# Retention blocks of a decoder step: the sample's state update moved behind the next block's low parts, and the last head's low parts moved to VectorE

## The chip, the core and the metric

The kernel runs on one core of a Trainium2 chip. The engines are TensorE (PE in the profile, PEld for its weight loads), VectorE (DVE), ScalarE (ACT), GpSimd (POOL) and SyncE (SP, which here only issues transfers). Each engine works through its own instructions in order and waits on semaphores. The metric is the device time of one execution in microseconds (us), as the median of three runs.

## What is computed

The reference is a decoder trunk of two layers for a prompt of 1024 positions and eight samples of one position. Layer 0 is windowed attention, layer 1 is retention, and each layer ends in a gated ConvFFN. The change touches the retention alone, and in it this recurrence (a chunk is 128 positions for the prompt, 1 for a sample; there are 4 heads, keys of 256 and values of 512):

```python
def step(s, inp):
    qi, ki, vi = inp
    inner = jnp.einsum('bihd,bjhd->bhij', qi, ki) * decay_in
    o = jnp.einsum('bhij,bjhe->bihe', inner, vi)
    o = o + jnp.einsum('bihd,bhde->bihe', qi, s) * q_decay[None, :, :, None]
    s = s * chunk_decay[None, :, None, None] + jnp.einsum('bjhd,bjhe->bhde', ki * k_decay[None, :, :, None], vi)
    return s, o
...
o = ((o - mu) * lax.rsqrt(var + GN_EPS)).reshape(b, t, nv)
out = (jax.nn.silu(g) * o).astype(x.dtype) @ w_o
```

The samples' states `state_ret` (8 samples, 4 heads, 256 x 512 each) are decayed, get the outer product of key and value added, go back to memory, and are multiplied with the sample's query.

## The kernel before, in words

Every large product is done in two parts: an operand is split into a high part (ScalarE, a copy that rounds) and a low part (VectorE or GpSimd, the operand less its high part), and TensorE adds three products: high x high, low x high, high x low.

The retention runs over 32 blocks `i` (head `h = i // 8`, chunk `n = i % 8`), and in block `i` one sample's state of that head is handled too: there are 8 samples and 8 chunks. Each engine has a function `period(i)`, in which the order of its work is written out by hand; `i` runs from 0 to 33, the last two without a live block. Between the block's own steps TensorE does filler jobs (a job is a product of 24 matmuls of 128 x 344 in blocks 0 to 15, in halves of 12, and of 12 such matmuls from block 16 on); `fill(i, s)` does those of slot `s`. From block 16 on a block has four or five jobs in turn.

TensorE in `period(i)`: `fill(i, 0)`; `inner(i)` (query times key; waits for the low parts of the key, `k_lo`); `back(i - 1)`; `update(i, 0)`; `fill(i, 1)`; `update(i, 1)` (waits until VectorE has taken up `update(i, 0)`); `fill(i, 2)`; `output(i)`; `turn(i + 1)` (the transposes of the next block); `fill(i, 3)`; `sample_out(i - 1)` (the sample's query times its new state, line 1359; waits for the semaphore `outer`); `fill(i, 4)`.

VectorE: the adds of finished jobs in the `fill` slots; `decayed(i)`, `gated(i - 1)`, `update(i, 0)`, `inner_lo(i)`, `update(i, 1)`; low parts of weight slabs in `split_planned` (line 2081), by a plan that says how many units each slot gets; `outer(i - 1)` (line 2752, two instructions of 128 x 512: state = value x key + state, both inputs in SBUF); `norm(i)` and `norm_rest(i)` (group norm of the block's output); `rows(i + 1)` (lines 2717 and 2719: the low parts of the next block's values and keys, `r_vl` and `r_kdl`); two more slots with adds and low parts of slabs.

ScalarE: `inner_hi(i)`; `decay(i)` (line 1926: the sample's state times its decay; waits for the load); high parts of slabs; `sample_state_out(i - 1)` (line 1938, issues the store of the state; waits for `outer`); `values_hi(i + 1)`; `state_hi(i)` (high parts of the prompt's state); more high parts of slabs (line 1428).

GpSimd: `heads_lo` (line 3094: low parts of finished heads `xl`, two instructions a call); `queries_lo(i + 1)`; `state_lo(i)` (line 3086: low parts of the prompt's state, 128 x 1024, both inputs in SBUF; not in the last chunk of a head).

SyncE loads the state of sample `i + 1` (`sample_state`, two buffers; waits for `sample_out` of the sample before and for the store that used the buffer) and the values (`sample_values`, one buffer) and then the next queries and values of the prompt.

Behind the blocks comes `last_chunks`: TensorE does two jobs, then `mean(6)` (line 839), which waits until GpSimd has added up eight tiles of `y` in `sums` (lines 3002 and 3005).

Of the kernel before, what the change touches and what calls it, by code (L numbers as in the profile page):

```python
# [459 lines left out]
def planned_slabs(i, k):  # L460
# [11 lines left out]
            "inv probs pt pt_in heads heads_hi heads_lo kv_out win_out s_sc s_scc "  # L472
            "s_tr s_mx s_ex s_p s_pt s_ptc s_o s_of s_oh s_ol dchain").split()
RET_SEMS = ("m_in dec_in cq0 cq1 cv cg0 cg1 turned q_hi q_lo v_hi v_lo k_hi k_lo inner inn i_hi i_lo kv state out_ "
            "s_hi s_lo stats small root ga back ob o_out o_hi o_lo st_in0 st_in1 st_out0 st_out1 decay outer "
            "x_in x_ing masks rows x_part x_sum xv xv_out vb x_o x_stats x_small x_root x_ga x_back xo xo_hi xo_lo "
            "s_out oin0 oin1 oin2").split()

# [1 line left out]
def own_columns(ch):  # L480

    return slice(ch * CH, min((ch + 1) * CH, SEQ))
# [315 lines left out]
def tensor_engine(pe, K):  # L798
# [461 lines left out]
    def ret_out(key):  # L1260

        h = key[1] if key[0] == "o" else RH - 1
        ch, ft = divmod(key[2], KT)
        s = S_O + 4 * h + ft // 2
        if ch == 0 and ft % 2 == 0:
            wait_slab(pe, S, s)
        if ft == 0:
            pe.wait_ge(R["o_lo"], 2 * (NCH * h + ch) + 2)
            if ch == NCH - 1:
                pe.wait_ge(R["xo_lo"], h + 1)  # L1270
        if key == ("o3", 0, 12):
            pe.wait_ge(R["state"], 2 * NI)
        free(key)
        c, out, terms = columns(ch), bank[BANK[key]][:, 0:CH], []
        for k in range(4):
            f = slice((2 * k + ft % 2) * P, (2 * k + ft % 2 + 1) * P)
            x = (4 * h + k) % KT
            w_hi, w_lo = unit_hi_lo(K, UNIT_OF_SLAB[s])
            terms.append((w_hi[:, f], w_lo[:, f], xh[:, x, c], xl[:, x, c]))
        accumulate(pe, out, terms).then_inc(S["jobs"], 1)  # L1280

    def fill(i, s):

        if i < MIXED:
            if s < 4:
                ret_half(FILL[i][s // 2 * 2 + 1][0], s % 2)
            return
        for key in FILL[i][s]:
            ret_out(key)
# [59 lines left out]
    def sample_out(i):  # L1349
        h, b = divmod(i, NB)  # L1350
        pe.wait_ge(R["masks"], h + 1)
        pe.wait_ge(R["outer"], 2 * i + 2)
        if b == 0:
            after(pe, R["x_sum"], h)
        for half in range(2):
            c = slice(half * RV // 2, (half + 1) * RV // 2)
            for j in range(2):
                at = 32 * (2 * half + j)
                mm = pe.matmul(xB[at:at + NS, c], K.qm[:, j, b, :], K.s0[:, i % 2, j, c], start=(b == 0), stop=(b == NS - 1))
        mm.then_inc(R["x_o"], 1)  # L1360
# [9 lines left out]
    def period(i):  # L1370
        h, n = divmod(i, NB)
        live = i < NI
        fill(i, 0)
        if live:
            inner(i)
        if 1 <= i <= NI:
            back(i - 1)
        if live:
            update(i, 0)
        fill(i, 1)  # L1380
        if live:
            update(i, 1)
            if n == 0:
                rows(h)
        if i in SAMPLES_BACK:
            sample_back(SAMPLES_BACK.index(i))
        fill(i, 2)
        if live:
            output(i)
        if i + 1 < NI:  # L1390
            turn(i + 1)
        fill(i, 3)
        if 1 <= i <= NI:
            sample_out(i - 1)
        fill(i, 4)

    for g in range(NG):
# [9 lines left out]
def scalar_engine(act, K):  # L1407
# [515 lines left out]
    def decay(i):  # L1923
        h = i // NB
        act.wait_ge(R[f"st_in{i % 2}"], 16 * (i // 2) + 16)
        act.activation(K.s0[:, i % 2, :, :], K.s0[:, i % 2, :, :], ACT.Copy, scale=K.dec[:, h % 2, W + 4:W + 5])\
            .then_inc(R["decay"], 1)
# [44 lines left out]
    def fill(jobs):  # L1972
        for key in jobs:
            if key[0] == "p":
                project(*key[1:])

    def period(i):
        h, n = divmod(i, NB)
        live = i < NI
        fill(FILL[i][0])  # L1980
        if live:
            inner_hi(i)
        if 1 <= i <= NI:
            gated_out(i - 1)
        if n == 1 and h:
            sample_parts(h - 1)
        if i == NI + 1:
            sample_root(RH - 1)
        fill(FILL[i][1])
        if live:  # L1990
            decay(i)
            if n == 0:
                sample_rows(h)
        if i in HEADS_SPLIT[:-1]:
            heads_hi(HEADS_SPLIT.index(i))
        if i < NI:
            split_planned(i, 1)
        elif FILL[i][1]:
            split_upto(J[FILL[i][1][-1]], U_F1)
        fill(FILL[i][2])  # L2000
        if 1 <= i <= NI:
            sample_state_out(i - 1)
        if n == 2 and h and live:
            sample_root(h - 1)
        if i in SAMPLES_PUT:
            sample_put(SAMPLES_PUT.index(i))
        if i == HEADS_SPLIT[-1]:
            heads_hi(len(HEADS_SPLIT) - 1)
        if live and n == NB - 1:
            state_out(h)  # L2010
        if i + 1 < NI:
            queries_hi(i + 1)
        if live:
            heads_root(i)
        if i + 1 < NI:
            values_hi(i + 1)
        if live and n < NB - 1:
            state_hi(i)
        if MIXED <= i < NI:
            split_planned(i, 2)  # L2020
        fill(FILL[i][3])
        if i < NI:
            split_planned(i, 3)
        fill(FILL[i][4])
        if i < NI:
            split_planned(i, 4)
        elif FILL[i][4]:
            split_upto(J[FILL[i][4][-1]], U_F1)
        if i == NI + 1:
            split_upto(J[FILL[i][3][-1]], U_F1 + 2)  # L2030
# [37 lines left out]
def vector_engine(dve, K):  # L2068
# [743 lines left out]
    def sample_put(h):  # L2812
        dve.wait_ge(R["xo_hi"], h + 1)
        k, c = sample_place(h)
        dve.tensor_tensor(xl[:, k, c], K.xo[:, :, :], xh[:, k, c].bitcast(F32), ALU.subtract).then_inc(R["xo_lo"], 1)

    def fill(jobs):
        for key in jobs:
            if key[0] == "p":
                project(*key[1:])  # L2820
            else:
                add(key)

    def period(i):
        h, n = divmod(i, NB)
        live = i < NI
        if i == NI + 1:
            sample_sums(RH - 1)
            sample_norm(RH - 1)
        fill(FILL[i][0])  # L2830
        if live:
            decayed(i)
        if 1 <= i <= NI:
            gated(i - 1)
        if live:
            update(i, 0)
            inner_lo(i)
        if i == NI + 1:
            sample_norm_rest(RH - 1)
        fill(FILL[i][1])  # L2840
        if live:
            update(i, 1)
        if n == 1 and live:
            if h:
                sample_sums(h - 1)
            masks(h)
        if n == 2 and h and live:
            sample_norm(h - 1)
        if i < NI:
            split_planned(i, 1)  # L2850
        elif FILL[i][1]:
            split_upto(J[FILL[i][1][-1]], U_F1)
        if 1 <= i <= NI:
            outer(i - 1)
        fill(FILL[i][2])
        if n == 2 and h and live:
            sample_norm_rest(h - 1)
        if i in SAMPLES_BACK:
            sample_gated(SAMPLES_BACK.index(i))
        if live:  # L2860
            norm(i)
        if i in SAMPLES_PUT:
            sample_put(SAMPLES_PUT.index(i))
        if live:
            norm_rest(i)
        if i + 1 < NI:
            rows(i + 1)
        if MIXED <= i < NI:
            split_planned(i, 2)
        fill(FILL[i][3])  # L2870
        if i < NI:
            split_planned(i, 3)
        fill(FILL[i][4])
        if i < NI:
            split_planned(i, 4)
        elif FILL[i][4]:
            split_upto(J[FILL[i][4][-1]], U_F1)
        if i == NI + 1:
            split_upto(J[FILL[i][3][-1]], U_F1 + 2)
# [54 lines left out]
def pool_engine(pool, K):  # L2934
# [161 lines left out]
    def period(i):  # L3096
        n = i % NB
        fill(FILL[i][0])
        if i in HEADS_SPLIT[:-1]:
            heads_lo(HEADS_SPLIT.index(i))  # L3100
        fill(FILL[i][1] + FILL[i][2])
        if i + 1 < NI:
            queries_lo(i + 1)
        if i < NI and n < NB - 1:
            state_lo(i)
        if i == HEADS_SPLIT[-1]:
            heads_lo(len(HEADS_SPLIT) - 1)
        fill(FILL[i][3] + FILL[i][4])

    pool.memset(K.eps[:, :], EPS).then_inc(S["e_in"], 1)  # L3110
# [43 lines left out]
def sync_engine(sp, K):  # L3154
# [193 lines left out]
    def period(i):  # L3348
# [8 lines left out]
            slabs_to(min(due_by(J[(FILL[i - 1][4] or FILL[i - 1][3])[-1]]), S_F1) + RAW)  # L3357
        if live:
            gates(i)
        if i == 14:  # L3360
            heads_written(8)
            sp.wait_ge(S["jobs"], J["p", 3, 11, 0])
            heads(0, 0)
# [32 lines left out]
        if i == 33:  # L3396
            heads_written(NI)
            heads_landed(2, 3)
            heads(3, 2)
        if i + 1 < NI:  # L3400
            sample_state(i + 1)
        if live:
            sample_values(i)
        if i == 15:
            sp.wait_ge(S["jobs"], J["p", 3, 11, 1])
            heads(0, 1)
# [209 lines left out]
```

## Time and profile before

| | us |
|---|---|
| median of three runs (lowest, highest) | 2744.42 (2742.86, 2746.85) |
| the profiled execution: its own time | 2740.04 |
| its span in the trace | 2738.0 |
| busy: PE | 2661.2 (97%) |
| busy: DVE | 1780.2 (65%) |
| busy: ACT | 1095.2 (40%) |
| busy: POOL | 767.0 (28%) |

A share is that of the span. Busy times add up each engine's own instructions; TensorE's matmuls overlap one another, so its row says when it had work and not how fast it was. A wait stands in the trace as the idle time in front of an instruction, with the instruction that ended it.

### The profile page before, as it was taken

What the parts mean: (1) busy time and instruction counts of PE and PEld (TensorE: products, weight loads), DVE (VectorE), ACT (ScalarE), POOL (GpSimd) and SP (SyncE); (2) the same over time, 40 slices, a digit from 0 to 9 for tenths busy, and PEclk for the clock granted to TensorE, in tenths of its full rate; (3) what the DMA queues carried; (4) which work ended last, traced back from release to release, by engine and by line L of the source; (5) the groups of instructions that cost most, each with busy time, mean ns of one, the idle gap of its engine ahead of it and who ended that gap; (6) DMA issues with size and microseconds to landing.
All of it is one profiled execution on the core that took longest, in us unless ns stands there. A gap on an engine that the chain in (4) does not pass through costs nothing.

```text
span 2738.0 us, 48829 instructions
## 1 busy us (share of the span) xinstructions
PE 2661.2 (97%) x19550; PEld 2549.9 (93%) x19550; DVE 1780.2 (65%) x3270; ACT 1095.2 (40%) x2089; POOL 767.0 (28%) x603
## 2 busy tenths in 40 slices
PE   8999989999999999999999999999899999999997
PEld 7888879999999999999999888898799999999997
DVE  6556578676767445766463675877688666766455
ACT  5445455433343122643434435433264444342123
POOL 3344351322220002354241232332341223220021
PEclk9999999999999999999999999999999999999999
DMA  4210111222224232123235777776502221223321
GB/s 141 82 48 11 40 33 55 70 86 78 84 79 155 70 116 65 67 93 122 96 109 173 220 233 220 232 224 199 162 22 73 82 82 70 86 96 123 114 73 62
DMA packets 182576, 290.83 MB, mean 106 GB/s; under 512 B 24976, under 2 KB 131088, under 8 KB 182320
## 3 DMA queue, kind: packets, MB, share of 16 engines
q1 hardware_dynamic: 152112, 251.65, 28.5%
q10 hardware_dynamic: 30240, 36.07, 3.7%
q8 instruction: 156, 2.56, 0.4%
q14 instruction: 68, 0.56, 0.1%
HBM read 206.82 MB, written 82.93 MB: 106 GB/s over the span
## 4 chain that ended last, share of the span: by engine, by line
PE 86%; DVE 6%; issue 3%; ACT 2%; POOL 1%; DMA 1%; ACTq 0%; SPq 0%; POOLq 0%; DVEq 0%
PE bank L1085 13%; PE bank L1087 13%; PE bank L1086 13%; PE bank L792 12%; PE bank L794 12%; PE bank L793 11%; PE bank L825 2%; PE bank L827 2%; PE bank L826 2%; PE bank L946 1%; PE bank L925 1%; DVE r_s L2752 1%; DVE wl L2081 1%; PE bank L936 1%; ACT wh L1428 0%
## 5 line engine op out<-in xcount | busy, mean ns | idle before, releaser
L2081 DVE TENSOR_TENSOR wl<-raw,wh 128x512 fp32r<-128x512 f32 (+1 forms) x460 | 428.9, 936 | 307.6 <-ACT wh L1428 302.5
L1428 ACT ACTIVATE wh<-raw 128x512 fp32r<-128x512 f32 (+1 forms) x492 | 344.3, 714 | 408.9 <-PE bank L794 224.7
L1085 PE MATMUL bank<-xh,wh 128*128 128x258 f32 x1792 | 506.7, 283 | 0.0
L1087 PE MATMUL bank<-xh,wl 128*128 128x258 f32 x1792 | 506.2, 282 | 0.0
L1086 PE MATMUL bank<-xl,wh 128*128 128x258 f32 x1792 | 505.5, 282 | 0.0
L1086 PEld LDWEIGHTS bank<-xl,wh 128*128 128x128 f32 x1792 | 338.7, 189 | 0.0
L1085 PEld LDWEIGHTS bank<-xh,wh 128*128 128x128 f32 x1792 | 338.2, 189 | 0.0
L1087 PEld LDWEIGHTS bank<-xh,wl 128*128 128x128 f32 x1792 | 337.9, 189 | 0.0
L2113 DVE TENSOR_TENSOR y<-bank,y 128x344 f32<-128x344 f32 x384 | 192.1, 512 | 218.4 <-PE bank L794 217.4
L3021 POOL TENSOR_TENSOR raw<-raw 128x512 f32<-128x512 f32 x56 | 72.1, 1287 | 742.8 <-DVE wl L2081 742.5
L1085 PE MATMUL bank<-x_t2h,wh 128*128 128x258 f32 x896 | 253.4, 283 | 2.0 <-ACT f_ab L1655 2.0
L1086 PE MATMUL bank<-x_t2l,wh 128*128 128x258 f32 x896 | 253.2, 283 | 0.0
L1087 PE MATMUL bank<-x_t2h,wl 128*128 128x258 f32 x896 | 252.7, 282 | 0.0
L1655 ACT ACTIVATE f_ab<-bank 128x258 f32<-128x258 f32 x224 | 86.1, 385 | 270.8 <-PE bank L1087 268.1
L1085 PEld LDWEIGHTS bank<-x_t2h,wh 128*128 128x128 f32 x896 | 169.1, 189 | 2.3 <-DVE wl L2081 2.3
L1087 PEld LDWEIGHTS bank<-x_t2h,wl 128*128 128x128 f32 x896 | 169.4, 189 | 0.0
L1086 PEld LDWEIGHTS bank<-x_t2l,wh 128*128 128x128 f32 x896 | 169.3, 189 | 0.0
L792 PE MATMUL bank<-xh,wh 128*128 128x344 f32 x488 | 163.0, 334 | 2.4 <-DVE f_cv L2392 1.5
L825 PE MATMUL bank<-xh,wh 128*128 128x344 f32 x472 | 156.4, 331 | 3.0 <-DVE xl L2150 2.3
L794 PE MATMUL bank<-xh,wl 128*128 128x344 f32 x488 | 157.0, 322 | 0.0
L793 PE MATMUL bank<-xl,wh 128*128 128x344 f32 x488 | 156.9, 321 | 0.0
L1655 ACT ACTIVATE f_g<-bank 128x258 f32<-128x258 f32 x224 | 84.1, 379 | 181.3 <-PE bank L1087 181.3
(308 smaller groups left out, 7192.8 us busy)
## 6 DMA issues: line engine op xcount, KB each, us to landing
raw<-in_w SPq DMA_DIRECT2D x216, 512.0 KB, 3.8
scratch_h<-f_g SPq DMA_DIRECT2D x40, 516.0 KB, 2.7
h_in<-scratch_h SPq DMA_DIRECT2D x30, 688.0 KB, 5.1
r_s<-in_state_in SPq DMA_DIRECT2D x32, 512.0 KB, 3.8
out_state_s<-r_s ACTq DMA_DIRECT2D x32, 512.0 KB, 3.5
scratch_qkvg<-f_ab SPq DMA_DIRECT2D x16, 516.0 KB, 4.1
scratch_qkvg<-f_g SPq DMA_DIRECT2D x16, 516.0 KB, 5.3
r_cxq<-scratch_qkvg SPq DMA_DIRECT2D x32, 256.0 KB, 5.4
```

Source lines behind the costliest of these rows:

```text
L792: pe.matmul(out, ah, bh, start=(k == 0), stop=False)
L793: pe.matmul(out, ah, bl, start=False, stop=False)
L794: mm = pe.matmul(out, al, bh, start=False, stop=(k == n - 1))
L825: pe.matmul(out, ah, xh[:, k, c], start=(k == 0), stop=False)
L1085: pe.matmul(out, hi[:, kk], bh, start=(k == 0 and not adds), stop=False, skip_group_check=adds)
L1086: pe.matmul(out, hi[:, kk], bl, start=False, stop=False, skip_group_check=adds)
L1087: mm = pe.matmul(out, lo[:, kk], bh, start=False, stop=(k == 3), skip_group_check=adds)
L1428: act.activation(hi, source, ACT.Copy).then_inc(S["hi_done"], 1)
L1655: act.activation(out, bank[PRODUCT_BANKS[sub][n]][:, 0:TQ], ACT.Copy).then_inc(S[f"copied{sub}"], 1)
L2081: dve.tensor_tensor(lo, source, hi.bitcast(F32), ALU.subtract).then_inc(S["lo_done"], 1)
L2113: dve.tensor_tensor(t, bank[b][:, 0:CH], t, ALU.add).then_inc(S["yadd"], 1)
L3021: pool.tensor_tensor(g[:, two], g[:, one], g[:, two], ALU.add).then_inc(S["w_sum"], 1)
```

## The change

The sample's part of a block is shifted, and the last low parts of the heads change their engine.

- VectorE: `outer(i - 1)` stands behind `rows(i + 1)`, no longer ahead of `norm(i)`.
- TensorE: `sample_out` stands in the next period, behind `fill(i, 0)` and ahead of `inner(i)`.
- ScalarE: `sample_state_out(i - 1)` and `decay(i)` stand behind slot 3, ahead of the slab parts of slots 3 and 4.
- SyncE: the state of sample `i` is loaded in period `i`, the values of sample `i - 1` in period `i` behind the gates.
- The last call of `heads_lo` goes from GpSimd to a new function `last_heads_lo` on VectorE, with a semaphore of its own, `o_end`. `sample_gated` stands ahead of the adds of slot 2.

```diff
@@ tensor engine, ret_out
         if ft == 0:
-            pe.wait_ge(R["o_lo"], 2 * (NCH * h + ch) + 2)
+            if (h, ch) == (RH - 1, NCH - 1):
+                pe.wait_ge(R["o_end"], 2)
+            else:
+                pe.wait_ge(R["o_lo"], 2 * (NCH * h + ch) + 2)
@@ tensor engine, period
         fill(i, 0)
+        if 2 <= i:
+            sample_out(i - 2)
         if live:
             inner(i)
...
         fill(i, 3)
-        if 1 <= i <= NI:
-            sample_out(i - 1)
         fill(i, 4)
@@ scalar engine, period
         fill(FILL[i][1])
-        if live:
-            decay(i)
-            if n == 0:
-                sample_rows(h)
+        if live and n == 0:
+            sample_rows(h)
...
         fill(FILL[i][2])
-        if 1 <= i <= NI:
-            sample_state_out(i - 1)
...
         fill(FILL[i][3])
+        if 1 <= i <= NI:
+            sample_state_out(i - 1)
+        if live:
+            decay(i)
         if i < NI:
             split_planned(i, 3)
@@ vector engine
+    def last_heads_lo():
+        n = NCH * RH - 1
+        for half in range(2):
+            k, c = slice(4 + 2 * half, 6 + 2 * half), own_columns(NCH - 1)
+            dve.wait_ge(R["o_hi"], 2 * n + half + 1)
+            dve.tensor_tensor(xl[:, k, c], xl[:, k, c].bitcast(F32), xh[:, k, c].bitcast(F32), ALU.subtract)\
+               .then_inc(R["o_end"], 1)
@@ vector engine, period
+        fill(FILL[i][0])
         if i == NI + 1:
             sample_sums(RH - 1)
             sample_norm(RH - 1)
-        fill(FILL[i][0])
...
-        if 1 <= i <= NI:
-            outer(i - 1)
+        if i in SAMPLES_BACK:
+            sample_gated(SAMPLES_BACK.index(i))
         fill(FILL[i][2])
         if n == 2 and h and live:
             sample_norm_rest(h - 1)
-        if i in SAMPLES_BACK:
-            sample_gated(SAMPLES_BACK.index(i))
         if live:
             norm(i)
         if i in SAMPLES_PUT:
             sample_put(SAMPLES_PUT.index(i))
+        if i == NI + 1:
+            last_heads_lo()
         if live:
             norm_rest(i)
         if i + 1 < NI:
             rows(i + 1)
+        if 1 <= i <= NI:
+            outer(i - 1)
         if MIXED <= i < NI:
             split_planned(i, 2)
@@ GpSimd, period
-        if i == HEADS_SPLIT[-1]:
-            heads_lo(len(HEADS_SPLIT) - 1)
@@ SyncE, period
         if live:
             gates(i)
+        if 1 <= i <= NI:
+            sample_values(i - 1)
...
-        if i + 1 < NI:
-            sample_state(i + 1)
-        if live:
-            sample_values(i)
+        if 1 <= i < NI:
+            sample_state(i)
```

VectorE in block 5, before (`r_il` is `inner_lo(5)`, `r_state` the second `update(5, 1)`, `r_s_145` the sample's state of `outer(4)`, `BN_STATS` the start of `norm(5)`):

```order
L2728 TENSOR_TENSOR r_il<-r_inn,r_ih 128x128 [waits r_i_hi]
L2742 SCALAR_TENSOR_TENSOR r_state<-r_state,r_dec,bank 128x512 [waits r_s_lo,r_kv]
L2752 SCALAR_TENSOR_TENSOR r_s_145<-r_vb,r_k_156,r_s_145 128x512 [waits r_vb,r_decay]
L2752 SCALAR_TENSOR_TENSOR r_s_145<-r_vb,r_k_156,r_s_145 128x512
L2768 BN_STATS r_st_139<-bank 128x6 [waits r_out_]
```

VectorE at the end of block 5 now (`r_vl` and `r_kdl` are the low parts of block 6's values and keys, `p_prod` the rotation of a filler job):

```order
L2785 TENSOR_SCALAR r_ga<-bank,r_st 128x512 [waits r_back,r_small]
L2720 TENSOR_TENSOR r_vl<-bank,r_vh 128x512 [waits r_v_hi]
L2722 SCALAR_TENSOR_TENSOR r_kdl<-bank,r_dec,r_kdh 128x256 [waits r_k_hi]
L2755 SCALAR_TENSOR_TENSOR r_s_145<-r_vb,r_k_156,r_s_145 128x512 [waits r_vb,r_decay]
L2755 SCALAR_TENSOR_TENSOR r_s_145<-r_vb,r_k_156,r_s_145 128x512
L2615 TENSOR_TENSOR p_prod<-bank,cosR 128x344 [waits rot,jobs]
```

The outer products have gone from ahead of the norm to between the low parts of the next block's keys and the filler's rotation.

TensorE at the end of block 4, before (`L1359` is `sample_out(3)`, the rows around it filler jobs):

```order
L827 MATMUL bank<-xh,wl 128x344
L1359 MATMUL bank<-r_s_145,r_qm 8x256 [waits r_outer,r_masks]
L1359 MATMUL bank<-r_s_145,r_qm 8x256 x3
L825 MATMUL bank<-xh,wh 128x344 [waits plain]
L826 MATMUL bank<-xl,wh 128x344
```

TensorE at the start of block 5 now (`L1362` is `sample_out(3)`, `L1315` `inner(5)`, `L1324` `back(4)`):

```order
L827 MATMUL bank<-xh,wl 128x344
L1362 MATMUL bank<-r_s_145,r_qm 8x256 [waits r_outer,r_masks]
L1362 MATMUL bank<-r_s_145,r_qm 8x256 x3
L1315 MATMUL bank<-r_cxq 128x128 [waits r_k_lo]
L1315 MATMUL bank<-r_cxq 128x128
L1324 MATMUL bank<-ident,r_ga 128x128 [waits r_v_lo,r_ga]
```

The product stands half a job (12 matmuls) later, directly ahead of `inner`; the outer products for which it waits now stand on VectorE behind the low parts for which `inner` waits.

ScalarE at the end of block 3, before (`r_sh` is `state_hi(3)`, `p_plain` a filler's result, `wh` the high part of a slab, `r_ih` `inner_hi(4)`):

```order
L1966 ACTIVATE r_sh<-r_state 128x1024 [waits r_out_,r_state]
L1783 ACTIVATE p_plain<-bank 128x344 [waits out_p1,jobs]
L1785 DMA scratch_qkvg<-p_plain 128x344 [waits plain]
L1428 ACTIVATE wh<-raw 128x1024 [waits jobs,raw_in0]
L1906 ACTIVATE r_ih<-r_inn 128x128 [waits r_inn]
```

ScalarE at the same place now (`L1941` is the store of the sample's state, `L1929` the decay):

```order
L1969 ACTIVATE r_sh<-r_state 128x1024 [waits r_out_,r_state]
L1786 ACTIVATE p_plain<-bank 128x344 [waits out_p1,jobs]
L1788 DMA scratch_qkvg<-p_plain 128x344 [waits plain]
L1941 DMA out_state_s<-r_s_145 128x1024 [waits r_outer]
L1929 ACTIVATE r_s_145<-r_s_145,r_dec 128x1024 [waits r_st_in1]
L1431 ACTIVATE wh<-raw 128x1024 [waits jobs,raw_in0]
L1909 ACTIVATE r_ih<-r_inn 128x128 [waits r_inn]
```

The store and the decay stand ahead of the slab's high part.

## Rows read from the trace of the kernel before

**Rows 1.** Waits of TensorE, 1495 to 2000 us: total us, times, longest us.

```profile
PE bank L839 <- POOLq L3009: 8.5, 1, 8.5
PE bank L1312 <- DVE r_kdl L2719: 6.2, 3, 3.6
PE bank L792 <- DVE r_state L2742: 5.9, 5, 1.7
PE bank L1304 <- DVE r_xo L2809: 2.8, 3, 1.3
PE bank L1359 <- DVE r_s L2752: 1.3, 1, 1.3
PE bank L1304 <- DMA r_cxq<-scratch_qkvg: 1.2, 1, 1.2
PE bank L792 <- issue: 0.9, 1, 0.9
PE bank L1367 <- DVE r_xv L2802: 0.3, 1, 0.3
```

**Rows 2.** Timeline, TensorE, blocks 6 and 7: start us, us, instruction [idle before].

```profile
1580.46 0.62 PE L1359 MATMUL bank<-r_s,r_qm 128*8 128x256 f32 x8
...
1582.99 0.60 PE L1312 MATMUL bank<-r_cxq 128*128 128x128 f32 x4
...
1586.45 0.39 PE L792 MATMUL bank<-r_vh,r_kdh 128*128 128x512 f32 x1
```

**Rows 3.** Timeline, VectorE, GpSimd and TensorE, from block 30 to block 31.

```profile
1936.47 0.47 DVE L2719 SCALAR_TENSOR_TENSOR r_kdl<-bank,r_dec,r_kdh 128x256 fp32r<-128x256 f32 x1
...
1936.54 2.40 POOL L3086 TENSOR_TENSOR r_sl<-r_state,r_sh 128x1024 fp32r<-128x1024 f32 x1 [1.99 <-ACT r_sh L1966]
...
1938.20 0.60 PE L1312 MATMUL bank<-r_cxq 128*128 128x128 f32 x4
```

**Rows 4.** Timeline, VectorE and GpSimd, blocks 30 and 31.

```profile
1930.00 1.41 DVE L2752 SCALAR_TENSOR_TENSOR r_s<-r_vb,r_k,r_s 128x512 f32<-128x512 f32 x2
...
1937.44 2.57 DVE L2081 TENSOR_TENSOR wl<-raw,wh 128x1024 fp32r<-128x1024 f32 x1 [0.49 <-ACT wh L1428]
...
1944.10 4.22 DVE L2752 SCALAR_TENSOR_TENSOR r_s<-r_vb,r_k,r_s 128x512 f32<-128x512 f32 x2
...
1944.01 3.75 POOL L3094 TENSOR_TENSOR xl<-xl,xh 128x688 fp32r<-128x688 f32 x2 [5.08 <-ACT xh L1917]
```

**Rows 5.** Timeline, VectorE and TensorE, block 29 with five jobs, into block 30.

```profile
1921.34 0.47 DVE L2719 SCALAR_TENSOR_TENSOR r_kdl<-bank,r_dec,r_kdh 128x256 fp32r<-128x256 f32 x1
...
1924.97 0.61 PE L1312 MATMUL bank<-r_cxq 128*128 128x128 f32 x4
```

**Rows 6.** Timeline, ScalarE, VectorE and TensorE, block 13.

```profile
1670.09 1.06 ACT L1428 ACTIVATE wh<-raw 128x1024 fp32r<-128x1024 f32 x1 [0.46 <-ACT p_plain L1783]
...
1674.58 1.15 ACT L1926 ACTIVATE r_s<-r_s,r_dec 128x1024 f32<-128x1024 f32 x1 [0.40 <-ACT p_plain L1783]
...
1671.18 1.22 DVE L2081 TENSOR_TENSOR wl<-raw,wh 128x1024 fp32r<-128x1024 f32 x1 [2.84 <-ACT wh L1428]
...
1674.01 0.47 PE L792 MATMUL bank<-r_vh,r_kdh 128*128 128x512 f32 x1 [1.32 <-DVE r_state L2742]
```

**Rows 7.** Timeline, GpSimd, the end of the blocks.

```profile
1968.75 4.28 POOL L3094 TENSOR_TENSOR xl<-xl,xh 128x672 fp32r<-128x672 f32 x2 [7.85 <-ACT xh L1917]
...
1975.03 6.16 POOL L3005 TENSOR_TENSOR n_ms<-n_ms,y 128x344 f32<-128x344 f32 x6
```

**Rows 8.** Windows on TensorE: stretch, us, busy (instructions), granted clock, DMA share, GB/s.

```profile
1640.60:1644.00 3.40, 3.40 (x13) 0.50 0.66 198
1715.70:1719.10 3.40, 3.40 (x13) 0.50 0.86 281
1763.60:1767.00 3.40, 3.38 (x20) 1.00 0.96 313
...
1981.30:1985.30 4.00, 4.00 (x12) 0.50 0.00 0
```

More of the change, by code:

```diff
@@ L474 @@
 RET_SEMS = ("m_in dec_in cq0 cq1 cv cg0 cg1 turned q_hi q_lo v_hi v_lo k_hi k_lo inner inn i_hi i_lo kv state out_ "
-            "s_hi s_lo stats small root ga back ob o_out o_hi o_lo st_in0 st_in1 st_out0 st_out1 decay outer "
+            "s_hi s_lo stats small root ga back ob o_out o_hi o_lo o_end st_in0 st_in1 st_out0 st_out1 decay outer "
             "x_in x_ing masks rows x_part x_sum xv xv_out vb x_o x_stats x_small x_root x_ga x_back xo xo_hi xo_lo "
```

## The prediction
> **What bounds the kernel now.** I read the page's busy times first: TensorE has work for 97% of the span, so a change in the order of the other engines can only move the idle time of TensorE. The view of who waited for whom on TensorE, for the stretch of the retention blocks, is therefore the budget [rows 1]: 8.5 us at `mean(6)`, where GpSimd's sums are late, and 18.6 us in the other seven rows, in waits of at most 3.6 us; 27.1 us in all. To that comes what the clock costs: behind the 8.5 us wait the granted clock is 0.50 (1.2 of 2.4 GHz) for 4.0 us, and it was 0.50 for 3.4 us in each of two stretches behind a wait for `r_kdl` [rows 8]. Work at half clock loses half its time, so these cost 2.0 + 1.7 + 1.7 = 5.4 us. Even if every one of these waits went and no new one came, 27.1 + 5.4 = 32.5 us is all that there is to win.
>
> Then I read the timeline of one boundary between two blocks on three engines, since the change puts a new link there. All times below count from k, the start of `r_kdl`, VectorE's last low part for the next block. TensorE begins `inner` at k + 1.73 (1938.20 less 1936.47), in a block with five jobs at k + 3.63 (1924.97 less 1921.34) [rows 3, 5]. GpSimd's `state_lo` begins at k + 0.07 and ends at k + 2.47 [rows 3]: exactly behind the low parts the port to SBUF is taken. What that does to VectorE is seen in two rows: the low part of a slab that starts in it takes 2.57 us and ends at 1940.01, 1.07 behind GpSimd's end; and two outer products beside two `heads_lo` instructions take 4.22 us where a pair alone takes 1.41, and end 0.56 behind GpSimd's end (1948.32 against 1947.76) [rows 3, 4]. So an instruction of VectorE with both inputs in SBUF makes hardly any way until GpSimd is done, and then needs most of its own time.
>
> **The change, part by part.** *The end of the blocks.* GpSimd loses its last `heads_lo`, 4.28 us ahead of the sums, of which six take 6.16 us in a row [rows 7]. Freed of it, it can add each tile soon after VectorE has added the job, one sum (1.03 us) per job of 1.9 us; the last sum then comes about a microsecond behind the last add, before TensorE has done its two jobs. The whole wait of 8.5 us and the 2.0 us of slow clock go. VectorE takes the low parts over; it waits there for jobs anyway, and TensorE needs `o_end` some nine jobs later: nothing.
>
> *The waits that go with the outer products.* They leave the place ahead of the norm, `sample_gated` moves ahead of an add, and queries are loaded earlier, since SyncE no longer stands at a wait for a late product. I let all of the other rows of the budget go, 18.6 us and 3.4 us of slow clock; where the same cause makes a wait again, it is counted below. Gain in all: 32.5 us.
>
> *The product now waits.* `sample_out` stands ahead of `inner` and takes some 0.6 us [rows 2], so TensorE comes to it at k + 1.73 - 0.6 = k + 1.13. The outer products follow `r_kdl`, inside `state_lo`. The first ends 0.56 behind it, at k + 3.03; the second adds 0.7 (half of 1.41): k + 3.73, and with some 0.1 for the semaphore TensorE goes on at k + 3.83. That is a wait of 2.7 us. Lower bound of this price: if GpSimd held nothing, the outer products would end at k + 0.4 + 1.41 = k + 1.8, and the wait would be 0.8. Upper bound: if each of the two were held as long as in the row of 4.22 us, they would end at k + 4.6 and the wait would be 3.6. I take 2.7, since `state_lo` is one instruction and can hold the pair but once. The plan of the jobs gives 21 boundaries of this kind (those with `state_lo` and four jobs, or two halves: from block 1 into 2 up to block 30 into 31): 21 x 2.7 = 56.7 us. Six boundaries follow a block with five jobs: TensorE comes at k + 3.63 - 0.6 and waits 0.8: 4.8 us. At two boundaries between heads there is no `state_lo`; the price is the lower bound, together 1.9 us. Sum 63.4 us. That the norm starts earlier without the outer products ahead of it helps little: in most blocks it waits for TensorE's output, and the boundary is counted from k in any case.
>
> Here a rule of the Trainium skill bears on the change. SBUF — State Buffer, section "Who interferes with whom", says that an instruction of VectorE with two SBUF inputs contends with a GpSimd instruction that reads SBUF, that whichever issues first keeps the shared ports for its whole length, and that the other one blocks fully. The rows agree for GpSimd ahead of VectorE; by the rule, the other order would hold `state_lo` instead, and the sum would be that of the first rival.
>
> *Store and decay ahead of the slab's high part.* ScalarE now waits for the outer products (k + 3.8), issues the store (0.4, the idle time that a store leaves in front of the decay), decays (1.15) and only then makes a high part of slots 3 and 4 (1.06) [rows 6]: ready at k + 6.4. VectorE's low part follows, and behind it stand `decayed`, `gated` and `update(i, 0)`, for which TensorE's second update waits: in block 13 it started 2.83 us behind the start of the low part [rows 6], so now at k + 9.3. Without that TensorE would be there 3.46 us behind `inner` [rows 2], at k + 3.83 + 0.6 + 3.46 = k + 7.9. A wait of 1.4 us at the five boundaries with a unit in slot 3 in the first half, 1.8 where an add lies between (three), 0.7 at the last of one head: 13.1 us. Below nothing it cannot fall; the upper end is the longest of the chain's own rows, 2.8 a time.
>
> *The last sample.* Its product stands one job later, with one job instead of two ahead of `sample_back`, which came only just too late before (0.3 us, [rows 1]). A job of 12 matmuls is 1.9 us (from the end of the product to `inner`, [rows 2]): 2.2 us.
>
> *Clock.* The 22 waits of 2.2 us and more are new, and the clock fell behind waits of 2.4 and 3.6 us, but not behind one of 1.7 [rows 1, 8]. One fall costs 1.7 us. Ends: none falls, 0; each falls, 37 us. These waits lie on the side of those with a fall, but each has a full block of work around it, so I take three in four: 28 us, less 5 where the slow stretch covers the 1.4 us wait for the slab: 23 us.
>
> *Nothing:* the load of a sample's state, though it moves a period back on SyncE. The store is issued at k + 3.8, and the next decay of that buffer stands a whole stretched block later; store and load take their turns in between. The loads of queries and values behind it on SyncE start earlier than before.
>
> **Sum.** 63.4 + 13.1 + 2.2 + 23 = 101.7 us lost, 32.5 us won: 69 us more. Against the profiled execution's own time of 2740.0 us that is 2809 us; the median of the runs lies 4.4 us above that execution, so I forecast 2814 us, 2.5% slower.
>
> **Rivals.**
> 1. *VectorE gets the port first.* If the outer products begin ahead of `state_lo`, GpSimd waits and not they. It decides itself by 0.33 us: `state_lo` would have to start behind k + 0.4 and not at k + 0.07. The price at the 21 boundaries falls to 0.8 us (16.8), at those with five jobs to nothing, and no clock falls: 16.8 + 1.9 + 13.1 + 2.2 - 32.5 = 1.5 us, so 2746 us, no change or just faster. Against it: `state_lo` hangs on ScalarE's `state_hi`, and ScalarE's order up to there is left as it was. Chance 0.09.
> 2. *No clock falls*: 69 - 23 = 46 us more, 2790 us. For it: 1.7 us did not do it [rows 8]. Chance 0.15; the other end, each wait with a fall, is 2822 us and part of the forecast.
> 3. *The sums stay late*, because VectorE's adds stand behind its new low parts and the slabs: the 10.5 us stay, 2824 us. Chance 0.08.
> 4. *The load becomes the bound*: store and load of one buffer would have to take over a whole block, and each block would grow by more: beyond 2842 us. Chance 0.04.
> 5. *The boundary moves ahead of TensorE.* I count from k; but VectorE no longer has the outer products (1.41) ahead of the norm, and if its low parts come 2.7 us earlier against TensorE than now, the product finds them done and only the end remains won: 10.5 us faster, about 2734 us. Against it: the keys' low part needs TensorE's transposes, and the norm its output, which VectorE cannot hasten. Chance 0.03.
>
> **How the numbers follow.** The forecast has the remaining 0.61. Its own bounds, with 0.3 us either way at 27 boundaries (8 us), reach from 2790 - 8 to 2822 + 8. I widen that a little for what the product's price leaves open (0.2 us a time are 4 us more): 2772 to 2842, which takes in rivals 2 and 3 and leaves out the first, fourth and fifth, 0.16. A measurement of this kernel tells 0.2% (5.5 us) from no change. Slower: 0.61 + 0.15 + 0.08 + 0.04 and a little of the first rival, 0.89; the same 0.06 and faster 0.05, from the first and fifth.
>
> **What would show it.** In the waits of TensorE the row of `mean(6)` is gone, and a row of the product (line 1362) waiting for the outer products (line 2755) stands in its place, some 29 times, with 2.7 us as the usual wait and some 60 us in all. The outer products behind `r_kdl` show 3 us and more for a pair. The second update waits for `r_state` up to 2 us at eight or nine boundaries, `sample_back` over 2 us. The granted clock falls to 0.50 many times between 1500 and 2050 us. I am wrong if the pairs show 1.4 us there, or if TensorE's sum of waits in that stretch is under 50 us.

## The result, and the profile after

| | before | changed |
|---|---|---|
| median of four runs, us (lowest, highest) | 2743.64 (2740.75, 2746.85) | 2814.88 (2809.99, 2818.03) |
| span of the profiled execution | 2738.0 | 2811.7 |
| TensorE busy in it | 2661.2 | 2687.4 |

The changed kernel takes 1.0257 times as long (95% interval 1.0243 to 1.0271): 71 us more. Forecast were 69 us more and 2814 us. So small a miss proves little; the terms have to be held against the rows one by one.

The page of the changed kernel, its span and the busy times (us, share of the span, instructions):

```profile
span 2811.7 us, 48832 instructions
...
PE 2687.4 (96%) x19550; PEld 2574.3 (92%) x19550; DVE 1809.5 (64%) x3272; ACT 1096.4 (39%) x2089; POOL 758.4 (27%) x601
```

TensorE has the same 19550 instructions as before and is busy 26.2 us longer. The same work took longer; that this is the clock is shown below, by the run in which TensorE was kept busy through its waits. The waits of TensorE in the stretch of the blocks, 1495 to 2070 us (line, what it waited for, total us, times, longest us), answer to [rows 1]:

```profile
PE bank L1362 <- DVE r_s L2755: 60.9, 27, 3.2
PE bank L1362 <- issue: 4.4, 3, 2.7
PE bank L1370 <- DVE r_xv L2805: 2.5, 1, 2.5
PE bank L792 <- DVE r_state L2745: 2.3, 2, 1.4
PE bank L792 <- DVE r_state L2749: 1.6, 2, 1.3
```

Of the eight rows of before three are left: `r_state` (5.9, now 3.9, in other blocks), `sample_back` (`r_xv`, 0.3, now 2.5) and the product (line 1362), which had 1.3 us and now has 60.9 + 4.4 = 65.3; its three waits under "issue" are of the same kind. The 8.5 us at `mean(6)` and the waits for `r_kdl`, `r_xo` and `r_cxq` are gone. Ahead of this stretch one wait has grown for which the forecast had no term: the first block's `inner`, 3.7 us where it was 1.5.

```profile
PE bank L1315 <- DVE r_kdl L2722: 3.7, 1, 3.7
```

It belongs to no part of the change that I can name: the kernels tried below had it at anything from 2.4 to 4.3 us, and one and the same kernel showed 2.4 and 3.2. What sets it stays open.

The account closes: waits 71.7 + 3.7 now against 27.1 + 1.5 before are 46.8 us more, and with 26.2 us of busy time that is 73.0 of the 73.7 us that the span has grown.

The timeline of one boundary, block 5 into 6, on VectorE, GpSimd, TensorE and ScalarE (start us, us, instruction, idle time before):

```profile
1586.35 0.47 DVE L2722 SCALAR_TENSOR_TENSOR r_kdl<-bank,r_dec,r_kdh 128x256 fp32r<-128x256 f32 x1
1586.42 2.37 POOL L3099 TENSOR_TENSOR r_sl<-r_state,r_sh 128x1024 fp32r<-128x1024 f32 x1 [2.00 <-ACT r_sh L1969]
1586.74 3.25 DVE L2755 SCALAR_TENSOR_TENSOR r_s<-r_vb,r_k,r_s 128x512 f32<-128x512 f32 x2
...
1590.15 0.84 PE L1362 MATMUL bank<-r_s,r_qm 128*8 128x256 f32 x8 [2.60 <-DVE r_s L2755]
1590.45 1.15 ACT L1929 ACTIVATE r_s<-r_s,r_dec 128x1024 f32<-128x1024 f32 x1 [4.10 <-DVE r_s L2755]
```

This is the link that the forecast described: k is 1586.35, GpSimd's low part of the state begins 0.07 later, and the pair of outer products takes 3.25 us and ends at k + 3.64 (forecast k + 3.73). TensorE waits 2.60 us. And the clock, as windows on TensorE (stretch, us, busy and instructions, granted clock, DMA share, GB/s), first the blocks of the kernel before, then the changed kernel:

```profile
1500.00:1990.00 490.00, 462.33 (x2911) 0.98 0.68 211
...
1500.00:2040.00 540.00, 471.82 (x2826) 0.94 0.59 189
...
1590.41:1593.81 3.40, 3.40 (x19) 0.50 0.64 234
1655.27:1662.10 6.83, 6.17 (x27) 0.50 0.40 129
```

Right behind the wait that ended at 1590.15 the granted clock is 0.50, 1.2 GHz, for 3.4 us; over the whole stretch it is 0.94 where it was 0.98 before. The same view behind each of the product's 21 waits of 2.6 to 3.2 us shows such a fall in 16 places. In three of them, the last row above among them, the clock stays at 0.50 for 6 us and more. Behind the other five waits, all of 2.60 to 2.62 us, it stays at 1.00; what decides between them is open.

### The profile page after: what moved, and what is told of

It reads as the page before. It is cut to its first block, busy times and chain, and to the rows that moved or that the text cites. A ratio compares the mean times of both kernels' runs of the same rounds, so it can differ in the third digit from the quotient of the medians.

```text
span 2811.7 us, 48832 instructions
## 1 busy us (share of the span) xinstructions
PE 2687.4 (96%) x19550; PEld 2574.3 (92%) x19550; DVE 1809.5 (64%) x3272; ACT 1096.4 (39%) x2089; POOL 758.4 (27%) x601
## 4 chain that ended last, share of the span: by engine, by line
PE 83%; DVE 10%; issue 3%; ACT 2%; DMA 1%; POOL 1%; SPq 0%; ACTq 0%; POOLq 0%; DVEq 0%
PE bank L1085 13%; PE bank L1087 13%; PE bank L1086 13%; PE bank L792 12%; PE bank L794 11%; PE bank L793 11%; DVE r_s L2755 3%; PE bank L825 2%; PE bank L827 2%; PE bank L826 2%; PE bank L1315 1%; PE bank L946 1%; PE bank L925 1%; PE bank L1362 1%; DVE r_vl L2720 1%
## 5 line engine op out<-in xcount | busy, mean ns | idle before, releaser
L2084 DVE TENSOR_TENSOR wl<-raw,wh 128x512 fp32r<-128x512 f32 (+1 forms) x460 | 422.5, 922 | 309.0 <-ACT wh L1431 303.2
```

The source lines that it names most:

```text
L2084: dve.tensor_tensor(lo, source, hi.bitcast(F32), ALU.subtract).then_inc(S["lo_done"], 1)
```

## The experiments

A ratio is to the kernel before, run in the same comparison. Over the five comparisons the median of the kernel before was 2742.51 to 2744.57 us, so medians of kernels from different comparisons are also set beside each other here. Some 0.2% (5.5 us) can be told from nothing. Diffs are against the changed kernel, where nothing else is said.

### The end of the blocks alone

The kernel before, with `last_heads_lo` on VectorE in place of GpSimd's last call, and TensorE's wait for `o_end`; nothing of the shift.

```diff
         if i in SAMPLES_PUT:
             sample_put(SAMPLES_PUT.index(i))
+        if i == NI + 1:
+            last_heads_lo()
...
-        if i == HEADS_SPLIT[-1]:
-            heads_lo(len(HEADS_SPLIT) - 1)
```

> The kernel before, with nothing of the change but the last head's low parts on VectorE. My account: the wait of 8.5 us for the sums goes, and with it the 2.0 us of slow clock behind it; some 10.5 us faster, 2733 us. Rival (the sums stay late because VectorE's adds stand behind its new low parts): the wait keeps its 8.5 us, 2744 us.

Measured 2734.23 us, ratio 0.9971 (0.9958 to 0.9984); in a second comparison, below, 2736.62 and 0.9976 (0.9966 to 0.9985): 9 and 6 us faster. The wait at `mean(6)` is gone from the waits, and the sums do not stay late. Not all of the 10.5 us arrive: the wait at `sample_back` grows from 0.3 to 1.6 us, and those for `r_kdl`, the first block included, from 7.7 to 10.0.

### What holds the outer products

```diff
     def state_lo(i):
         pool.wait_ge(R["s_hi"], rows_of_state(i) + 1)
+        after(pool, R["outer"], 2 * i)
```

> The changed kernel, in which GpSimd's state_lo waits for the outer products, so that the two cannot overlap; all else as it is. Port account: the pair takes 1.4 us instead of 3.2, the product waits 0.8 us at 21 boundaries instead of 2.6 (39 us less) and the clock hardly falls (some 25 to 30 us less): about 2750 us. Rival (they are slow by themselves): 2815 us, the pair at 3.2 us.

Measured 2748.91 us, ratio 1.0016 (1.0007 to 1.0026), as my account had it. One added wait on GpSimd gives back 66 us. A boundary in this run (timeline; the columns as above):

```profile
1592.02 0.47 DVE L2722 SCALAR_TENSOR_TENSOR r_kdl<-bank,r_dec,r_kdh 128x256 fp32r<-128x256 f32 x1
1592.41 1.40 DVE L2755 SCALAR_TENSOR_TENSOR r_s<-r_vb,r_k,r_s 128x512 f32<-128x512 f32 x2
...
1593.96 2.39 POOL L3100 TENSOR_TENSOR r_sl<-r_state,r_sh 128x1024 fp32r<-128x1024 f32 x1 [3.87 <-DVE r_s L2755]
1593.96 0.62 PE L1362 MATMUL bank<-r_s,r_qm 128*8 128x256 f32 x8 [0.76 <-DVE r_s L2755]
```

Same instructions, same place on VectorE: 1.40 us instead of 3.25, a wait of 0.76 instead of 2.60. The rival is out: the outer products are not slow by themselves. The forecast's lower bound for the product, 0.8 us, is what stands here. The waits of TensorE in this run, over the same stretch as above:

```profile
PE bank L1362 <- DVE r_s L2755: 21.7, 23, 1.5
PE bank L792 <- DVE r_state L2745: 8.1, 7, 1.7
...
PE bank L1362 <- issue: 0.8, 1, 0.8
```

The product waits 21.7 + 0.8 = 22.5 us instead of 65.3, and TensorE's busy time is 2659.3 us instead of 2687.4: the slow clock went with the long waits. `r_state` shows more than in the changed kernel (8.1 us in seven waits, where its line 2745 has 2.3 in two); that comes up again below.

The other test of the same link moves VectorE's instructions instead of GpSimd's:

```diff
+        if 1 <= i <= NI:
+            outer(i - 1)
         if i + 1 < NI:
             rows(i + 1)
-        if 1 <= i <= NI:
-            outer(i - 1)
```

> The changed kernel, with the outer products directly ahead of the next block's low parts instead of behind them. If GpSimd's instruction is what holds them, they now run ahead of it, the pair takes 1.4 us, the product never waits, inner waits some 0.3 us at 21 boundaries and the clock does not fall: about 2720 us, 24 faster than before. If only the first of the two gets through and the second is held, r_kdl comes some 2.4 us later than now and inner waits 2.5 us in place of the product: about 2814 us. Rival (an outer product is slow there by itself, 2.6 us, whatever GpSimd does): inner waits 1.6 us at 21 boundaries, 2750 to 2760 us.

Measured 2788.09 us, ratio 1.0163 (1.0146 to 1.0180): far from the 2720 us that I put first, and below the second case. The timeline of this run shows why, at the ends of block 5 and of block 9:

```profile
1586.90 3.58 DVE L2755 SCALAR_TENSOR_TENSOR r_s<-r_vb,r_k,r_s 128x512 f32<-128x512 f32 x2
1587.57 2.37 POOL L3099 TENSOR_TENSOR r_sl<-r_state,r_sh 128x1024 fp32r<-128x1024 f32 x1 [2.00 <-ACT r_sh L1969]
...
1590.63 0.62 PE L1362 MATMUL bank<-r_s,r_qm 128*8 128x256 f32 x8 [1.95 <-DVE r_s L2755]
...
1647.24 1.41 DVE L2755 SCALAR_TENSOR_TENSOR r_s<-r_vb,r_k,r_s 128x512 f32<-128x512 f32 x2
1648.05 2.84 POOL L3099 TENSOR_TENSOR r_sl<-r_state,r_sh 128x1024 fp32r<-128x1024 f32 x1 [2.20 <-ACT r_sh L1969]
```

In the first, GpSimd begins 0.67 us behind the pair's start, in the instant between its two halves, and the pair takes 3.58 us: one half free, the other held. In the second it begins 0.81 behind, 0.14 later; the pair takes its 1.41 and GpSimd is the one that is stretched, to 2.84. The product still waits, 40.3 us in 20 places, and `inner` some 0.3 at each boundary. So the case "only the first gets through" happened at most boundaries, but I had priced it too high: the held half takes 2.9 us and delays the product by 1.95, which stands ahead of `inner` and takes the wait on itself.

By the Trainium skill (SBUF — State Buffer, section "Who interferes with whom") the engine that issues first holds the ports and the other blocks. The traces agree in both directions: 3.25 us for a pair behind GpSimd's start, 2.84 us for GpSimd behind the pair's second half.

### What the clock costs

Products that nobody reads keep TensorE busy in its wait for the outer products.

```diff
         fill(i, 0)
+        if 2 <= i < NI and i % NB and (i - 1 < MIXED or not FILL[i - 1][4]):
+            pe.wait_ge(R["k_lo"], i + 1)
+            for _ in range(16):
+                pe.matmul(inner_bank[:, 2 * W:3 * W], ident[:, :], ident[:, :], start=True, stop=True)
```

> The changed kernel, with 16 products of 128x128 that nobody reads on TensorE in front of the sample's product, at the boundaries where it waits 2.6 us; they lie inside that wait. If a good part of the loss is the clock that falls behind the idle stretch, the falls go and nothing else does: 26 us of TensorE's busy time less, some 5 us of waits for r_state that stood in slow stretches more: about 2790 us. Rival (the idle time itself is the whole loss): 2815 us or a little more.

Measured 2803.71 us, ratio 1.0221 (1.0205 to 1.0236), between my two values. I had made the filling too long: the 16 took 3.7 us of a wait of 2.6, so this run mixes a gain and a loss. With 11 in their place:

> As the run with 16 idle products on TensorE, with 11. The 16 took 3.7 us (1586.57 to 1590.24), about 1.0 longer than the wait that they were to fill, at 21 boundaries; 11 take 2.5 us. If the clock costs what TensorE's busy time grew by (26 us), this one takes 2790 to 2795 us. Rival (the run with 16 shows the true gain, 11 us, and its products cost nothing): 2804 us again.

Measured 2790.89 us, ratio 1.0173 (1.0158 to 1.0189), as expected. Its timeline, windows and waits of TensorE:

```profile
1585.42 2.62 PE L1380 MATMUL bank<-ident 128*128 128x128 f32 x22
...
1588.19 0.62 PE L1362 MATMUL bank<-r_s,r_qm 128*8 128x256 f32 x8 [0.15 <-DVE r_s L2759]
```

```profile
1500.00:2030.00 530.00, 504.36 (x3339) 1.00 0.61 194
```

```profile
PE bank L1362 <- DVE r_s L2759: 11.8, 27, 1.3
PE bank L792 <- DVE r_state L2749: 7.6, 7, 1.4
...
PE bank L792 <- DVE r_state L2753: 1.6, 2, 1.3
```

The product comes as late as in the changed kernel (k + 3.80 in both), but the granted clock is 1.00 over the stretch and the kernel is 24 us faster than the changed one. Without the 21 x 2.62 us of idle products, TensorE's 2711.1 us of busy time here are 31.3 us less than in the changed kernel (2687.4 + 55.0 - 2711.1). Most of the difference between the 31 and the 24 stands in the third of these views: `r_state` now costs 7.6 + 1.6 = 9.2 us in nine waits, where the changed kernel shows 3.9 in four. A TensorE at half clock comes late to the second update, and the slab's delay does not show. The changed kernel bears this out: behind the product in the five blocks that lack the wait the granted clock is 0.50 to 0.70 over 3.4 us, in the four that have it 1.00. One of the four is block 4, VectorE's `r_kdl` (k) and TensorE's second update:

```profile
1553.20 0.47 DVE L2722 SCALAR_TENSOR_TENSOR r_kdl<-bank,r_dec,r_kdh 128x256 fp32r<-128x256 f32 x1
...
1562.23 0.47 PE L792 MATMUL bank<-r_vh,r_kdh 128*128 128x512 f32 x1 [0.97 <-DVE r_state L2745]
```

### The product later

```diff
         fill(i, 0)
-        if 2 <= i:
+        if i == NI + 1:
             sample_out(i - 2)
...
         fill(i, 1)
+        if 2 <= i <= NI:
+            sample_out(i - 2)
         if live:
             update(i, 1)
```

> The changed kernel, with the sample's product half a block later on TensorE, behind the second filler of the block (ahead of the second update), where the outer products are long done; VectorE, ScalarE and GpSimd as in the change. My account: all waits of the product but the last go, and the falls of the clock with them. But TensorE then reaches the second update at k + 5.3, and r_state is ready only at k + 8.5 in the nine blocks with a slab's unit behind store and decay (8.4 in the changed kernel's block 4): waits of 3.2 us there, 29 us, with a fall behind some of them, 10 us: about 2750 us. Rival (the wait for the product was all, and the slab's delay is nothing by itself): 2712 to 2720 us.

Measured 2787.78 us, ratio 1.0157 (1.0140 to 1.0174). Both expectations were too low. The waits of TensorE in this run:

```profile
PE bank L792 <- DVE r_state L2747: 45.0, 21, 4.3
...
PE bank L792 <- DVE r_state L2751: 3.2, 2, 2.7
...
PE bank L1362 <- DVE r_s L2757: 1.1, 1, 1.1
```

Of the product's waits only the last is left, and the second update waits instead, in 23 blocks and not in nine. Added up from the timeline, the nine wait 29.6 us, as expected; the other 14, which I had at nothing, wait 18.6, some 4 of which the kernel before had too. The slow clock costs more than the 10 us expected: TensorE is busy 2680.7 us, 24.6 more than in the run with 11 idle products without these. One of the 14, without a slab's unit, on VectorE and then on TensorE:

```profile
1573.96 3.27 DVE L2757 SCALAR_TENSOR_TENSOR r_s<-r_vb,r_k,r_s 128x512 f32<-128x512 f32 x2
...
1578.85 0.28 DVE L2729 TENSOR_TENSOR r_inn<-bank,r_dec 128x128 f32<-128x128 f32 x1
1579.05 0.68 DVE L2739 TENSOR_TENSOR r_ob<-bank,r_cxg 128x512 f32<-128x512 f32 x1
1579.64 0.73 DVE L2747 SCALAR_TENSOR_TENSOR r_state<-r_state,r_dec,bank 128x512 f32<-128x512 f32 x1
...
1580.52 0.47 PE L792 MATMUL bank<-r_vh,r_kdh 128*128 128x512 f32 x1 [1.75 <-DVE r_state L2747]
```

The 3.27 us stand on VectorE itself, ahead of the filler's rotation and all that follows in the next block. The product was only the first that met the late outer products; without it the next in line waits.

On top of that, store and decay behind the slab's high part:

```diff
+        if i < NI:
+            split_planned(i, 3)
         if 1 <= i <= NI:
             sample_state_out(i - 1)
         if live:
             decay(i)
-        if i < NI:
-            split_planned(i, 3)
```

> As the one before, and on ScalarE the store and the decay stand behind the slab's high part of slot 3 instead of ahead of it. My account: the high part is ready in time, the low part follows the outer products at once (k + 3.7 to k + 4.9), r_state is ready at k + 6.5 and the nine waits shrink from 3.2 to about 1.2 us, without falls: about 2725 us. Rival (store and decay are not what delays r_state): the same time as the one before.

Measured 2752.48 us, ratio 1.0036 (1.0023 to 1.0049): 35 us less, more than the 25 expected. The waits of TensorE for `r_state`:

```profile
PE bank L792 <- DVE r_state L2747: 31.2, 21, 3.1
...
PE bank L792 <- DVE r_state L2751: 1.2, 2, 0.7
```

The nine blocks with a slab shrank from 29.6 to 13.9 us in all (block 4 from 3.83 to 1.20; two of the nine did not shrink), while the 14 others kept theirs, 18.4 us. The rest of the gain is that with the long waits most falls of the clock went too: TensorE's busy time is 2662.4 us, and 2680.7 in the run before. The time itself, 2752 us, misses the 2725 us expected, since the 14 blocks were not in the account. With `state_lo` held back in addition:

> All three moves: the product late, store and decay behind the slab's high part, and GpSimd's state_lo behind the outer products. If the outer products are out of the way at k + 1.9, the slab's low part ends at k + 3.1 and r_state is ready at about k + 5: no waits at the nine blocks, 2712 to 2716 us, some 30 us under the kernel before. Against it: state_lo now runs from k + 1.9 to k + 4.3, into the slab's low part, which has two SBUF inputs too; then that one is held, r_state comes at k + 6.5 as in the run without it, and the time is about 2725 us.

Measured 2739.81 us, ratio 0.9985 (0.9975 to 0.9994), above both values expected. The objection in the expectation came true, as the end of block 9 shows on VectorE and GpSimd:

```profile
1631.33 2.03 DVE L2086 TENSOR_TENSOR wl<-raw,wh 128x1024 fp32r<-128x1024 f32 x1
...
1629.87 2.42 POOL L3102 TENSOR_TENSOR r_sl<-r_state,r_sh 128x1024 fp32r<-128x1024 f32 x1 [3.94 <-DVE r_s L2757]
```

The slab's low part takes 2.03 us instead of 1.23, because GpSimd's instruction has been moved into it. Waits of 16.6 us for `r_state` remain on its line 2747. Not held back, GpSimd's instruction meets the outer products; held back, it meets the slab's low part.

### The outer products back, the rest of the shift kept

```diff
         elif FILL[i][1]:
             split_upto(J[FILL[i][1][-1]], U_F1)
+        if 1 <= i <= NI:
+            outer(i - 1)
         if i in SAMPLES_BACK:
...
-        if 1 <= i <= NI:
-            outer(i - 1)
         if MIXED <= i < NI:
```

> The changed kernel with one part undone: VectorE's outer products stand ahead of the norm again, as in the kernel before. Product, store, decay, loads and the end of the blocks stay as in the change. My account: the place of the outer products behind the low parts, where GpSimd holds them, is what costs; here the pair takes 1.4 us, the product one step later finds them done and never waits, the clock falls three times or less, and the end's 10 us stay won. Left: r_kdl (6 to 10 us, as with the end alone), r_state with the decay ahead of the slab's high part (6 to 15 us), 2.5 us at sample_back: 2735 to 2745 us. Rival (product, store, decay and loads a step later cost by themselves, some 65 us with the clock): 2790 us or more.

Measured 2750.86 us, ratio 1.0023 (1.0014 to 1.0033), 64 us under the changed kernel; a little above my bounds, far from the rival. With ScalarE's order turned as above, in addition:

> As the one before, and on ScalarE store and decay behind the slab's high part of slot 3. My account: r_state waits shrink to the 5.9 us of the kernel before or less: 2728 to 2736 us, as good as the end alone or a little better. Rival (the order on ScalarE does not matter here): the same as the one before.

Measured 2740.31 us, ratio 0.9990 (0.9980 to 0.9999). The order on ScalarE is worth 10.5 us; but the time is above what I expected and above the end alone. What was left was `r_kdl` (in all 14.5 us), and the view of the outer products' own line names its cause: what VectorE waited for ahead of them (us, times).

```profile
its engine sat idle before it (us, times) until:
  DMA r_vb<-scratch_rows: 31.7, 12
```

The change loads a sample's values only in the block in which they are used. So the last of these kernels, beside the two edits above, puts that load back; with it the end alone was run again:

```diff
-        if 1 <= i <= NI:
-            sample_values(i - 1)
...
         if 1 <= i < NI:
             sample_state(i)
+        if live:
+            sample_values(i)
```

> As the run with the outer products back ahead of the norm and store and decay behind the slab's high part, and the load of a sample's values back at its old place, at the end of the block before. In that run VectorE's outer products waited 31.7 us in 12 places for these values, and inner waited 14.5 us for r_kdl behind them. My account: those waits of r_vb go, r_kdl falls to the 6 to 8 us of the kernel before or less: 2728 to 2734 us, beside 2734 for the end alone. Rival (the values were late beside something else that binds): 2740 us again.

> The end alone a second time, for a comparison on the same chip: 2733 to 2736 us. If the rest of the shift is worth anything once the outer products stand ahead of the norm and the values come early, the run before is below this one; if not, it is not.

Measured 2727.14 us, ratio 0.9938 (0.9921 to 0.9954), just below the range expected, beside 2736.62 us for the end alone. Its largest waits of TensorE, from 1480 us on, the first block included:

```profile
PE bank L1315 <- DVE r_kdl L2722: 7.2, 4, 3.9
PE bank L792 <- DVE r_state L2745: 6.4, 6, 1.7
PE bank L1370 <- DVE r_xv L2805: 2.6, 1, 2.6
```

VectorE no longer waits for the values. This is the best version found, 15 us below the kernel before: product and decay a step later, outer products and values where they were.

## Why the prediction was right, point by point

- **The end of the blocks** (10.5 us won): the mechanism was right; alone it gave 6 to 9 us.
- **The waits that go** (the other rows of the budget): right for the rows that the forecast named. The first block's 2.2 us more was not in it.
- **The product** (63.4 us): 65.3 us, by the mechanism that was forecast, shown by holding GpSimd back. The 21 boundaries came to 57.4 (forecast 56.7): the usual wait is 2.6, and four, into blocks 12 to 15, are 3.2. The six behind five jobs came to 4.7 (4.8), the two between heads to 2.1 (1.9; twice the bound of 0.8 would be 1.6). The last sample's product waits 1.2 us more, which the forecast did not count.
- **Store and decay ahead of the slab's part** (13.1 us): the chain was right, its size too high, and most of the rows that it foretold do not appear. The run with the clock held up has all nine waits, and they cost 9.2 us, some 0.4 less each than forecast: in block 4 `r_state` let TensorE go on at k + 9.0 and not 9.3, and TensorE came at k + 8.1 and not 7.9. The changed kernel shows four of them, 3.9 us; the slow clock hides the other 5.3. The forecast had seen this, and took 5 us off for it, but from the price of the clock.
- **The clock** (28 us less those 5; 5.4 gone): the run with 11 idle products puts it at 31.3 us. Three in four of 22 waits were to bring a fall, and 17 did, the last sample's among them; the price of one fall, 1.7 us, was too low for the three where the clock stayed at 0.50 for 6 us and more. The two terms together were forecast as 13.1 + 28 - 5 = 36.1 us and came to 9.2 + 31.3 - 5.3 = 35.2. That is luck in part: one was 3.9 us too high, the other 3.3 too low.
- **The last sample** (2.2 us): 2.5 us.
- **Nothing for the loads**: right for the sample's state; in the changed kernel no decay waits for its load. Of the sample's values the forecast said nothing. They too are loaded later, and that was free only because the outer products stood late: in the run with these ahead of the norm and ScalarE's order turned, VectorE waited 31.7 us for them.
- **The rivals**: VectorE ahead of GpSimd was to give 2746 us; with GpSimd made to wait, 2748.91 us were measured. GpSimd came 0.07 behind k, at three boundaries 0.2, so the condition of that rival was not met. But the condition, a start behind k + 0.4, was set too low: in the run with the outer products first GpSimd started 0.67 us behind the pair's start at most boundaries and still held its second half.

What the forecast did not see is that the product was not the only one in line. It counted the delay where TensorE meets it first. In the run with the product later the second update waits 18.6 us in blocks where the order on ScalarE has no part, because VectorE's own chain is late.

## What to carry to other kernels

Before an instruction is moved on VectorE, look at what GpSimd does at the new place: here, with both inputs in SBUF, a pair of 1.4 us became 3.2 us behind a GpSimd instruction of 2.4 us that started 0.3 us earlier. A wait that an experiment takes away should be looked for at the next consumer before its price is called saved. Waits and slow clock are to be priced together: here 65 us of waits at the block boundaries brought some 31 us of slowed work with them, and the slowed work hid 5 us of other waits.

## What the runs showed that I had not expected

- Where GpSimd's instruction started in the instant between two VectorE instructions that follow one another, it usually went first. In the run with the outer products first, `state_lo` started 0.66 to 0.68 us behind the start of a pair at 24 boundaries, and at 22 of them the second half was held, 2.9 us in place of 0.74. At the other two, and at the three with a start 0.8 us behind, the pair took 1.4 us and GpSimd 2.84 to 2.97.
- Eleven products that nobody reads, 2.6 us at each of 21 waits, made the kernel 24 us faster. They removed no wait; they kept the granted clock at 1.00 where it had been 0.94.
